# First attention of a fused two-block transformer kernel: transpositions, copies and values one step later, four mLSTM units in flight, three banks for transposed rows of its softmax half

## What is computed

```
hm  = mlstm_chunkwise(mq, mk, m_v, m_i, m_f)       # 4 heads of 128: decayed q.k products times v
hm  = sigmoid(m_o) * rms_norm(hm)
mla = softmax(causal(q . k * scale)) @ v           # 4 heads: q, k of 128 + 64 rotary columns
mix = concatenate([mla, hm]) @ w_out
```

## Time and profile before

| | |
|---|---|
| median of 3 runs (lowest to highest) | 1326.5 us (1322.2 to 1328.2) |
| the profiled execution: its time, its span | 1326.6 us, 1324.3 us |
| mean granted clock of the matmul engine | 0.994 |
| first attention: from its first score to the first matmul of out1 | 122.80 to 217.63 us |

### The profile page before, as it was taken

The page is one execution under the profiler, slowest core; times in us unless marked ns, Lnnn a source line. Parts: engine busy times, 40 slices in busy tenths (PEclk is TensorE's granted clock), DMA queues, the critical chain, the costliest instruction groups (busy, mean ns, idle before and its releaser), DMA issues.

```text
span 1324.3 us, 17570 instructions
## 1 busy us (share of the span) xinstructions
PE 1288.7 (97%) x6460; PEld 1086.2 (82%) x6460; DVE 769.2 (58%) x1237; ACT 550.3 (42%) x909; POOL 43.8 (3%) x45
## 2 busy tenths in 40 slices
PE   9999989999999999999989999999999999999997
PEld 7887887998888888888868888788897788888886
DVE  6876676566444443333775896786876622355334
ACT  5556565343222223322544655566543222222221
POOL 4000000000000000000030000000000000000002
PEclk9999999999999999999999999999999999999999
DMA  5232102112222233323223332322212232222322
GB/s 193 89 102 66 32 33 96 64 50 94 95 95 96 97 101 119 111 95 111 95 97 96 96 96 80 104 73 82 78 49 80 96 99 98 89 95 96 112 95 80
DMA packets 37067, 119.91 MB, mean 91 GB/s; under 512 B 4492, under 2 KB 6668, under 8 KB 37008
## 3 DMA queue, kind: packets, MB, share of 16 engines
q1 hardware_dynamic: 35744, 116.93, 27.3%
q0 software_dynamic: 544, 1.58, 0.4%
q10 hardware_dynamic: 720, 0.60, 0.1%
HBM read 111.74 MB, written 2.11 MB: 86 GB/s over the span
## 4 chain that ended last, share of the span: by engine, by line
PE 81%; DVE 13%; ACT 3%; issue 2%; ACTq 0%; DVEq 0%
PE bank L874 25%; PE bank L875 25%; PE bank L876 25%; DVE w_lo L2083 3%; DVE tiles L2083 2%; DVE tiles L2086 1%; DVE arena L2083 1%; PE bank L975 1%; DVE negmax L2298 1%; PE bank L1050 1%; ACT w_hi L1494 1%; DVE arena L2086 1%; DVE probsT L2083 1%; DVE residual L2083 1%; ACT arena L1511 1%
## 5 line engine op out<-in xcount | busy, mean ns | idle before, releaser
L2083 DVE TENSOR_TENSOR w_lo<-raw_slab,w_hi 128x1024 fp32r<-128x1024 f32 x198 | 245.2, 1239 | 279.4 <-ACT w_hi L1494 278.3
L874 PE MATMUL bank<-u_hi,w_hi 128*128 128x512 f32 x824 | 325.3, 395 | 6.9 <-DVE w_lo L2083 2.8
L876 PE MATMUL bank<-u_hi,w_lo 128*128 128x512 f32 x824 | 322.3, 391 | 0.0
L875 PE MATMUL bank<-u_lo,w_hi 128*128 128x512 f32 x824 | 322.2, 391 | 0.0
L1494 ACT ACTIVATE w_hi<-raw_slab 128x1024 fp32r<-128x1024 f32 x198 | 208.7, 1054 | 181.5 <-PE bank L876 177.1
L874 PE MATMUL bank<-arena,w_hi 128*128 128x512 f32 (+1 forms) x692 | 262.1, 379 | 5.1 <-DVE u_lo L2083 2.5
L875 PE MATMUL bank<-arena,w_hi 128*128 128x512 f32 (+1 forms) x692 | 259.8, 375 | 0.0
L876 PE MATMUL bank<-arena,w_lo 128*128 128x512 f32 (+1 forms) x692 | 259.6, 375 | 0.0
L874 PEld LDWEIGHTS bank<-u_hi,w_hi 128*128 128x128 f32 x824 | 155.4, 189 | 41.8 <-DVE w_lo L2083 4.5
L876 PEld LDWEIGHTS bank<-u_hi,w_lo 128*128 128x128 f32 x824 | 155.4, 189 | 32.9
L875 PEld LDWEIGHTS bank<-u_lo,w_hi 128*128 128x128 f32 x824 | 155.6, 189 | 30.3
(11 more groups left out here) (259 smaller groups left out, 1512.9 us busy)
## 6 DMA issues: line engine op xcount, KB each, us to landing
raw_slab<-in_stream SPq DMA_DIRECT2D x198, 512.0 KB, 3.3
aside_raw<-in_stream SPq DMA_DIRECT2D x8, 512.0 KB, 5.1
arena<-arena SPq DMA_DIRECT2D x32, 128.0 KB, 2.3
residual<-in_xT SPq DMA_DIRECT2D x8, 256.0 KB, 6.4
out_hT<-residual SPq DMA_DIRECT2D x12, 128.0 KB, 1.7
arena<-forget_rows SPq DMA_DIRECT2D x8, 128.0 KB, 2.3
tiles<-in_pT POOLq DMA_DIRECT2D x2, 256.0 KB, 3.0
tiles<-bias_rows POOLq DMA_DIRECT2D x1, 512.0 KB, 4.6
```

What stands on the lines that cost most here:

```text
L874: pe.matmul(o, ws[0], xs[0], start=first, stop=False)
L875: pe.matmul(o, ws[0], xs[1], start=False, stop=False)
L876: return pe.matmul(o, ws[1], xs[0], start=False, stop=last)
L2083: return nc.vector.tensor_tensor(o, a, b, op)
```

## The change

It does five things, all in the first attention. (1) The lags of transposition, low copy and PV become 4, 5 and 6 in this pass and stay 3, 4 and 5 in the others; heads and the end of the loop follow (LAG_HEAD 10, LAG_TAIL 7), so the pass has 39 steps, and PV stands in odd steps. (2) mLSTM products take slot v mod 4 and the exps of mLSTM go to two other tiles (SQ, SQ+1), so four units are in flight: the product of unit v waits for the transposition of unit v-4. (3) ACT's special waits before the first four softmax exps go; they wait like the others for the transposition of the unit four before. (4) Transposed rows of softmax units rotate through banks 3, 4 and 6. (5) Values of softmax heads have bank 5 alone, as bank 6 is taken by (4). Fills, conversions and rotary splits keep their steps.

```diff
--- before.py
+++ after.py
@@ -223,9 +223,10 @@
     _h += HEADS[_name] if _name != "ml" else 0
 NEXP = _e
 
-LAG_EXP, LAG_NORM, LAG_T, LAG_LO, LAG_PV = 1, 2, 3, 4, 5
-LAG_HEAD = LAG_PV + ST
-LAG_TAIL = LAG_PV + 1
+LAG_EXP, LAG_NORM = 1, 2
+LAG_T, LAG_LO, LAG_PV = ({g: lag + (g == "first") for g in PASSES} for lag in (3, 4, 5))
+LAG_HEAD = {a: LAG_PV[g] + ST for g in PASSES for a in PASSES[g]}
+LAG_TAIL = {g: LAG_PV[g] + 1 for g in PASSES}
 DF_SPREAD_BANKS = (0, 1, 2, 7)
 CONVERT_BEFORE = {1: 7, 2: 8, 4: 9, 6: 10, 8: 11, 10: 12}
 PAIR_START, PAIR_COLS = (0, 3 * P), 11 * P
@@ -273,13 +274,13 @@
     return (df_tiles(h) if key[0] == "d" else FX_TILES[h])["low"]
 
 PROB, MO, TMP, SSUM, SQ, RSTD, NTILES = 0, 4, 8, 10, 11, 13, 14
-PT_BANKS, STAT_BANK = (3, 4), 7
+PT_BANKS, STAT_BANK = {"ml": (3, 4), "mla": (3, 4, 6), "df": (3, 4), "fx": (3, 4)}, 7
 SCORE_BANKS = {"ml": (0, 1, 2, 6), "mla": (0, 1, 2), "df": (0, 1, 2, 6), "fx": (0, 1, 2)}
 ML_SCORES = {}
 for _u in range(ML_H * ST):
     for _j in range(1 if _u % ST < ST // 2 else 2):
         ML_SCORES[_u, _j] = SCORE_BANKS["ml"][len(ML_SCORES) % len(SCORE_BANKS["ml"])]
-CTX_BANKS = {"ml": (5,), "mla": (5, 6), "df": (5,), "fx": (5, 6)}
+CTX_BANKS = {"ml": (5,), "mla": (5,), "df": (5,), "fx": (5, 6)}
 
 
 def at(n, it, per):
@@ -351,7 +352,7 @@
             use(key, STAT_BANK, slab(key), (sem.projected, PROJECTED.index(key) + 1))
 
     def attention(g):
-        for step in range(units_of(g) + LAG_TAIL):
+        for step in range(units_of(g) + LAG_TAIL[g]):
             if fill_begun(g, step):
                 fill(fill_begun(g, step))
         for v in range(units_of(g)):
@@ -372,7 +373,7 @@
                 else:
                     uses["score", a, u, 1] = (ML_SCORES[u, 0], None, (sem.score_ready, n + 1))
             n = UNIT0[a] + u
-            use(("pT", a, u), PT_BANKS[n % 2], (sem.pT_ready, n + 1), (sem.pT_lo, n + 1))
+            use(("pT", a, u), PT_BANKS[a][u % len(PT_BANKS[a])], (sem.pT_ready, n + 1), (sem.pT_lo, n + 1))
             if u % ST == ST - 1:
                 n = HEAD0[a] + u // ST
                 free = {"ml": (sem.sq_done, SQ0["ml"] + u // ST + 1), "df": (sem.ctx_read, u // ST + 1)}
@@ -667,15 +668,13 @@
 
         def prob_slot(a, v):
 
-            if a == "ml":
-                return (2 * v + 1) % 4
             if a == "df":
                 return (2 * v) % 8
             return v % 4
 
         def exp_slot(a, v, j):
             if a == "ml":
-                return (2 * v) % 4
+                return SQ - PROB + v % 2
             if a == "df":
                 return (2 * v + j) % 8
             return v % 4
@@ -1035,8 +1034,8 @@
 
 
                 units, unit0 = units_of(g), UNIT0[PASSES[g][0]]
-                for step in range(units + LAG_TAIL):
-                    v = step - LAG_T
+                for step in range(units + LAG_TAIL[g]):
+                    v = step - LAG_T[g]
                     if 0 <= v < units:
                         a, n = unit_at(g, v)
                         i = v % ST
@@ -1052,7 +1051,7 @@
                     if step < units:
                         a, n = unit_at(g, step)
                         score[a](n, n // ST, n % ST)
-                    v = step - LAG_PV
+                    v = step - LAG_PV[g]
                     if 0 <= v < units and v % 2:
                         a, n = unit_at(g, v)
                         h, i = n // ST, n % ST
@@ -1574,21 +1573,18 @@
             def attention(g, softmax, head, filled=None, convert=None):
 
                 units, unit0 = units_of(g), UNIT0[PASSES[g][0]]
-                for step in range(units + LAG_TAIL):
+                for step in range(units + LAG_TAIL[g]):
                     v = step - LAG_EXP
                     if 0 <= v < units:
                         a, n = unit_at(g, v)
-                        if a == "mla" and n < 4:
-                            act.wait_ge(sem.gated, ML_H * ST - (n == 0))
-                            act.wait_ge(sem.pT_ready, unit0 + ML_H * ST - (n < 3))
-                        elif a != "ml" and n >= 4:
+                        if a == "mla" or a != "ml" and n >= 4:
                             act.wait_ge(sem.pT_ready, unit0 + v - 4 + 1)
                         for j in range(PER_UNIT[a][1]):
                             softmax[a](n, n // ST, n % ST, j)
                     key = fill_ended(g, step - 1)
                     if key and filled and g == "first":
                         filled(key)
-                    v = step - LAG_T
+                    v = step - LAG_T[g]
                     if 0 <= v < units:
                         a, n = unit_at(g, v)
                         w = (v % ST + 1) * P
@@ -1728,7 +1724,7 @@
             def plain_head(a, rows):
 
                 def run(step):
-                    h = at_head(a, step, LAG_HEAD)
+                    h = at_head(a, step, LAG_HEAD[a])
                     if h is not None:
                         r, tile = rows(h)
                         nc.scalar.activation(arena[r, MIX_HI + tile], full(act, ("ctx", a, h))[r, :], ACT.Copy).then_inc(sem.mix_hi, 1)
@@ -1742,7 +1738,7 @@
                     n = ROTARY_SPLIT[step]
                     act.wait_ge(sem.rope_added, 2 + n)
                     stacked_hi(f"qpe{n}", A_QPE[2 * n:2 * n + 2], t(TMP), MLA_SCALE)
-                h = at_head("ml", step, LAG_HEAD)
+                h = at_head("ml", step, LAG_HEAD["ml"])
                 if h is not None:
                     o = full(act, ("ctx", "ml", h))
                     if h == ML_H - 1:
@@ -2255,12 +2251,12 @@
             def attention(g, normalise, maxima, head, taken, split=None, convert=None):
 
                 units, unit0 = units_of(g), UNIT0[PASSES[g][0]]
-                for step in range(units + LAG_TAIL):
+                for step in range(units + LAG_TAIL[g]):
                     v = step - LAG_NORM
                     if 0 <= v < units:
                         a, n = unit_at(g, v)
                         normalise[a](n)
-                    v = step - LAG_LO
+                    v = step - LAG_LO[g]
                     if 0 <= v < units:
                         a, n = unit_at(g, v)
                         w = (v % ST + 1) * P
@@ -2509,8 +2505,8 @@
                 e = EXP0["ml"] + v
                 o = full(dve, ("score", "ml", v, 1))
                 dve.wait_ge(sem.exp_done, e + 1)
-                if v >= 2:
-                    dve.wait_ge(sem.pT_ready, UNIT0["ml"] + v - 1)
+                if v >= 4:
+                    dve.wait_ge(sem.pT_ready, UNIT0["ml"] + v - 3)
                 p = tiles[:, PROB + prob_slot("ml", v), 0:w]
                 stt(p, o[:, ml_products(i)], 1.0, tiles[:, PROB + exp_slot("ml", v, 0), 0:w], ALU.mult, ALU.mult,
                     accum_out=rowsum[:, e:e + 1]).then_inc(sem.gated, 1)
@@ -2734,7 +2730,7 @@
                 return stt(p0, p0, rowinv[:, e:e + 1], p1, ALU.mult, ALU.subtract)
 
             def df_head(step):
-                h = at_head("df", step, LAG_HEAD)
+                h = at_head("df", step, LAG_HEAD["df"])
                 if h is not None:
 
                     o = full(dve, ("ctx", "df", h))
```

## The result

The changed kernel takes 1329.5 us (median of nine runs, 1327.8 to 1330.7); the kernel before, in the nine runs beside them, 1325.8. The ratio is 1.0031, 95% interval 1.0021 to 1.0041: slower by 0.3%, less than the half per cent that one measurement tells from no change, but nine runs a side tell it from none. The forecast was 1329.5.

What follows compares the result with a forecast made beforehand. PE, busy 97%, was taken as the bound. Waits summed to 15.2 us against 10.8 (+4.4), but +2.9 from walked starts was taken: 1326.6 + 2.9 = 1329.5 us; forecast case 1326 to 1332, range 1321.5 to 1334.3.

Steps and rivals of the forecast that it cites:

- step 5: Transposition wait of 1.47 us in step 5 becomes 1.05 at a score plus 0.1 at the next transposition: 1.15 us.
- v3: Fill in step 8, losing 1.46 us of values in front of it: 0.7 us of new wait.
- qn1: Fill in step 14, losing 0.79 us of values in front of it: 0.35 us of new wait.
- kn3: Fill in step 20, losing 1.46 us of values in front while DVE's split comes late: wait 3.1 us instead of 0.90.
- mlstat: Statistics matmul in step 24, losing 1.46 us of cover: wait 1.5 us instead of 0.17.
- mlnorm1 to 3: Fills behind the statistics, where DVE sets the pace: waits of 3.35 us together instead of 2.82.
- values of step 31: A softmax head's first values wait for the previous head's low half on the single bank: 1.5 us, bounds 0 and 2.
- output fill: First projection fill, step 32, waits bare for DVE's last low half of the mLSTM rows: 1.35 us.
- +4.4: First attention: the PE waits summed term by term, 15.2 us after the change against 10.8 before.
- +2.9 from starts walked through the steps: First attention's end by walked starts: 218.85 against 217.63, +1.2 without a clock fall, +2.9 with the same fall; adopted.
- The cover of fills: Values moving to odd steps change the work in front of fills, 1.46 or 0.79 us each, shortening or lengthening their waits.
- The rival in which waits only change their name: First attention: transposition waits pass to scores and fills on the same DVE instructions, cancelling out: 1326.6 us, chance 0.20.

Runs made afterwards that it cites:

- e7: The changed kernel with four fills and the second weight conversion shifted a step, so no fill needing a split follows another in the next even step: 1328.3 us, 1.0026.
- e2: The kernel before with only the change's banks (three for softmax transposed rows, bank 5 alone for softmax heads' values), old lags and slots: 1324.7 us, 0.9995.
- e8: e7 with the first half of output fill 0 waiting for the low halves of two mLSTM heads instead of four: 1326.3 us, 1.0011.
- e3: The changed kernel with the old banks again (two for transposed rows, 5 and 6 in turn for softmax heads' values): 1329.5 us, 1.0036.
- e12: The kernel before with only the values of unit 19 moved from in front of the statistics to behind them: 1327.2 us, 1.0016.
- e5: The changed kernel with fills kn2 and kn3 one step earlier and kn2's split counted before the rotary split: 1328.2 us, 1.0020.
- e6: The changed kernel with everything except scores, exps and normalisations one step later from step 7 on: 1330.6 us, 1.0042.
- e9: The kernel before with the change's banks, and both rotary splits, the second weight conversion and two fills moved to other steps: 1325.6 us, 0.9999.
- e11: The kernel before with the change's banks, fill kn2 in step 18, split before the rotary split, and second weight conversion in step 11: 1323.9 us, 0.9993.

## Why the forecast held, and where its steps did not

**Time and sign** were right, and the mechanism was the one forecast in outline: no transposition waits, new waits of the same size behind the same DVE instructions, and in the second part DVE late by what stands in front. That the time came out to the tenth of a us is luck. The forecast was 1326.6 + 2.9, all of the 2.9 from the schedule at an equal clock; measured are 1325.8 + 3.7, of which about 1 to 2 us are schedule and the rest goes with a lower clock (below). Nothing moved outside the stretch by more than a fall.

**Term by term.** Forecast and measured: qpe1 0.63, 0.64; score of step 3, 0.74, 0.76; step 5, 1.15, 0.76; v3 0.7, 0.89; qn1 0.35, 0.36; kn3 3.1, 2.86; qn2 0, 0; mlstat 1.5, 1.22; mlnorm1 to 3 3.35, 2.59; values of step 31, 1.5, 0.35; output fill 1.35, 1.14; and DVE's new wait for the score of unit 26, 1.4, 1.52. The 0.15 at qn0, 0.3 behind head 3 and 0.4 in the drain did not come. Sum 15.2 against 11.57. So the sum of waits was too high by 3.6 us, and the +4.4 made from it was a poor estimate; the +2.9 from starts walked through the steps, a walk that the prediction does not write out, was the better one. The stretch grew by 2.08 with 3.4 us more at the lower level in it. Put together from parts without a fall, it grew by 1.8: 60.45 (the change) and 34.63 (e7, with the same order there) against 61.31 and 32.00 (e2).

**The term most off** is the wait on the single bank of values. In the changed kernel it is 0.35 because PE, at half clock in that profile, arrived late. Without a fall it is 1.14 (e7) and 1.13 (e8), still under the 1.5 of the DVE sum. Booking it beside the output fill's was right: without a fall both stand there, 1.14 and 1.15 (e7). But it does not show in the time: with the second bank back (e3) PE waits 0.58 and 0.96 at other places, and the ratio is 1.0036.

**What the sum did not see.** No matmul is added, so at a full clock the change costs what PE's waits grow by, and that comes out to within 0.4 us: without falls they grow by 2.2 us (7.49 and 4.88 against 6.19 and 4.02) and the stretch by 1.8. The sum booked +4.4 for it. It had the values of unit 19 in two of its terms, at mlstat and behind the statistics, and did not see that they are the one move behind most of the cost: they and a transposition, 2.19 us of PE's busy time, left a part that got only 0.86 us shorter without them. e12 shows the values alone, +1.6 us in the second part and 0.16% in time. At an equal mean clock they cost about 2.2 us (at 0.996 seven runs of e12 take 1326.7 on the mean, thirty-three of before 1324.5), no less than the whole schedule of the change, whose first part gains something elsewhere.

**The cover of fills** explains the size of single waits in the change (v3, qn1, kn3, mlstat all within 0.3 us), but not the time: e5 gave back a third of the wait at kn3, e7 nothing more, and e6 lost. The rival in which waits only change their name was, for the first part, nearer the truth than I gave it.

**The clock** got more of the loss than I allowed. I took one fall as before. In the profile it lasts 6.8 us instead of 3.4, and the rest of the kernel has one fall fewer. Over the runs the mean granted clock is 0.9930 (nine of the change) against 0.9955 (ninety-five of the kernel before, beside the experiments): 2 x 0.0025 x 1327 = 6.6 us more at half speed, at most 3.3 us if PE is the bound there. At an equal clock the change costs less than the 3.7 us between the medians: at 0.994 the means are 1328.0 (three runs) and 1326.9 (nine), at 0.993 1329.8 (three) and 1327.6 (three). So 1.1 to 2.2 us is schedule, and the rest goes with the clock; with three to nine runs a side, and a clock given to 0.001 (some 1.2 us), this split is a rough one. Why the changed kernel's runs have the lower clock stays open: no run here set the clock apart. By the same comparison e8 is level with before: four of its runs at 0.995 take 1325.9 on the mean, thirty-six of before 1325.8, and its 0.1% goes with four of its eleven runs lying at 0.993, where only three of the ninety-five of before lie.

In the ten profiles that have falls in this stretch, each begins within a wait of PE of 1.1 to 2.9 us or less than 2 us behind one, in e9 at the end of 1.81 us and 0.6 us behind 1.98. But e12, with waits of 1.81, 1.62 and 1.49 us, had none there, and neither had the change behind its 2.86. The Trainium skill says (TensorE: Matmul & The Clock Gate, A second HAM failure mode) that frequent short idles of the matmul engine between groups of matmuls bring such a back and forth of the clock. The traces agree in that much, and do not show when a wait has a fall behind it and when not.

**The third bank.** The Trainium skill (Perfetto Trace Analysis, Matmuls) asks that independent groups of matmuls rotate through different banks. By that the prediction had 1323.3. Without the lags, and with the values' second bank given up for it, the third bank took 1324.7 against 1325.7 for its kernel before (e2), not told from no change. It can reach one of the two waits counted there, as the 1.47 lies in the mLSTM half, which keeps two banks. The other it shortened by 0.5 us only, because the row to be transposed was ready only 0.6 us before the bank was free (in the kernel before, 205.36 and 205.96 us on DVE's timeline).

## What to carry to other kernels

Before a stage is moved by a step, look at what it now stands in front of: work moved out of a stretch that is paced by another engine hardly shortens it, and the same work lengthens the stretch that it enters. A wait that the profile names can be removed and its time not gained, when the same engine's next instruction is what the waiter needs next; price the second wait before the first is touched. Where single waits of 1 to 3 us are shifted about, the falls of the granted clock are as large as the schedule's own effect: here 3.4 us at the lower level went with a second part longer by 0.9 to 1.6 us (36.46 with 6.8 us against e7's 34.63 with none; e11's 33.57 with 3.4 against e2's 32.00). So compare kernels at the same mean clock too.

## What the runs showed that I had not expected

Falls of the granted clock came in pieces of 3.4 us or twice that in all fourteen profiles, never shorter inside a kernel, and the runs of one and the same kernel sort by their mean clock: the kernel before takes 1322.6 us on the mean at a mean clock of 0.997, 1325.8 at 0.995, 1327.6 at 0.993. Most of the spread of this kernel's ninety-five runs (1321.9 to 1328.5) goes with it: the mean clock accounts for four fifths of their variance.
